# Moving the block boundary and the general-pass branch into the middle of the experts of a two-block transformer kernel

## What is computed

```python
h = _rms_norm(x, norm_mix[i])
z = h @ w_in[i]                      # q, k, v, conv inputs cu, cg, gates ga, gb
...
merged = jax.nn.sigmoid(ga) * y_a + jax.nn.sigmoid(gb) * y_b
x = x + merged @ w_out[i]
h2 = _rms_norm(x, norm_ffn[i])
x = x + _hier_moe(h2, ...)           # 32 experts, width 512, two of one group per token
g_ple = jax.nn.sigmoid(_rms_norm(x, norm_ple[i]) @ w_ple_gate[i])
x = x + g_ple * (p[i] @ w_ple_proj[i])
```

## Time and profile before

| | us |
|---|---|
| median of 3 runs | 2069.28 |
| lowest, highest | 2068.17, 2074.96 |
| profiled execution, its own time | 2068.92 |
| its span in the profile | 2066.8 |

### The profile page before, as it was taken

The page is one execution under the profiler, slowest core; times in us unless marked ns, Lnnn a source line. Parts: engine busy times, 40 slices in busy tenths (PEclk is TensorE's granted clock), DMA queues, the critical chain, the costliest instruction groups (busy, mean ns, idle before and its releaser), DMA issues. The chain is left out here.

```text
span 2066.8 us, 21051 instructions
## 1 busy us (share of the span) xinstructions
PE 1727.0 (84%) x9170; PEld 1120.7 (54%) x9170; DVE 545.8 (26%) x1109; ACT 335.2 (16%) x695; POOL 0.2 (0%) x4
## 2 busy tenths in 40 slices
PE   7999967666665899998666576679999999999999
PEld 6788522212221787883222122147888877888744
DVE  3853200000000376431000000025566333210000
ACT  2231200000000222310000000012152244210000
POOL 0000000000000000000000000000000000000000
PEclk9999987888888999999888878889999999999999
DMA  8436699999999634359999999981433333333441
GB/s 341 163 133 248 279 427 428 427 429 426 429 427 428 256 131 155 134 233 408 427 428 426 428 428 428 428 344 70 157 132 137 125 109 95 122 142 143 163 162 62
DMA packets 40175, 560.97 MB, mean 271 GB/s; under 512 B 4464, under 2 KB 4464, under 8 KB 5744
## 3 DMA queue, kind: packets, MB, share of 16 engines
q1 hardware_dynamic: 40080, 559.57, 66.7%
HBM read 558.50 MB, written 1.05 MB: 271 GB/s over the span
## 5 line engine op out<-in xcount | busy, mean ns | idle before, releaser
L1182 PE MATMUL ps<-ring,hB 128*32 128x512 f32 x1344 | 196.0, 712 | 119.7 <-DMA ring<-in_stream 119.7
L1574 PE MATMUL ps<-hA,ring 128*128 128x256 f32 (+1 forms) x1312 | 289.2, 382 | 0.6 <-DVE b_sc L2202 0.6
L1574 PEld LDWEIGHTS ps<-hA,ring 128*128 128x128 f32 (+1 forms) x1312 | 246.4, 188 | 42.2 <-issue 4.6
L563 PE MATMUL ps<-hA,ring 128*128 128x256 f32 x1152 | 253.0, 380 | 0.0
L563 PEld LDWEIGHTS ps<-hA,ring 128*128 128x128 f32 x1152 | 217.7, 190 | 32.7 <-issue 3.7
L1182 PEld LDWEIGHTS ps<-ring,hB 128*32 128x32 f32 x1344 | 41.7, 121 | 271.3 <-DMA ring<-in_stream 135.8
L1182 PE MATMUL ps<-l_extra,hB 128*32 128x512 f32 x704 | 117.5, 802 | 82.5 <-DMA l_extra<-in_stream 82.5
L1193 PE MATMUL ps<-ring,l_work 128*32 128x512 f32 x704 | 106.0, 736 | 55.7 <-DMA ring<-in_stream 47.2
L1274 DVE TENSOR_TENSOR l_work<-ps,l_work 128x512 f32<-128x512 f32 x16 | 11.1, 692 | 436.5 <-ACT l_work L1248 436.5
L1182 PEld LDWEIGHTS ps<-l_extra,hB 128*32 128x32 f32 x704 | 23.0, 128 | 163.5 <-DMA l_extra<-in_stream 93.4
L1836 PE MATMUL ps<-ring 128*128 128x512 f32 x256 | 110.0, 592 | 0.0
(11 more groups left out here) (317 smaller groups left out, 1696.3 us busy)
## 6 DMA issues: line engine op xcount, KB each, us to landing
ring<-in_stream SPq DMA_DIRECT2D x189, 2048.0 KB, 37.6
l_extra<-in_stream SPq DMA_DIRECT2D x64, 2048.0 KB, 40.8
ring<-in_stream SPq DMA_DIRECT2D x6, 1792.0 KB, 16.6
ring<-in_stream SPq DMA_DIRECT2D x4, 1344.0 KB, 7.9
ring<-in_stream SPq DMA_DIRECT2D x2, 1764.0 KB, 9.0
ring<-in_stream SPq DMA_DIRECT2D x2, 1024.0 KB, 29.8
b_bias<-in_bias SPq DMA_DIRECT2D x1, 2048.0 KB, 12.9
xT<-in_xT SPq DMA_DIRECT2D x1, 1024.0 KB, 4.8
```

What stands on the lines that cost most here:

```text
L563: mm = self.nc.tensor.matmul(out[:, m * T:(m + 1) * T], w[:, k, c * P:(c + 1) * P], src[:, k, :], start=(k == 0), stop=(k == kc - 1))
L1182: mm = nc.tensor.matmul(out[js, :], x_slots[q % 2][:, c, js], w[:, 0, j * D + n0:j * D + n0 + FF], start=(c == 0), stop=(c == DC - 1))
L1574: mm = nc.tensor.matmul(out[0:width, m * T:(m + 1) * T], w[:, k, (c0 + m) * width:(c0 + m + 1) * width], src[:, k, :], start=(k == 0), sto ...
```

## The change

The order of the program becomes: block 0 with the front of layer 0 and its quads 0 to 3; clear, load and branch; block 1 with the quads 4 to 7 and the PLE stage of layer 0, the front of layer 1 and its quads 0 to 3; clear, load and branch; block 2 with the rest of layer 1 and its PLE stage; clear; the second block of the model. There are as many boundaries as before. In detail:

- `SPLIT` is 4. `moe_tensor`, `moe_scalar` and `moe_vector` take a range of quads and a running number `n` for the semaphore counts within a block. At a boundary SP has issued the first eight slabs of the next quad and no more, since the two slots behind them serve `over_block` as scratch.
- The PLE slab stands in the stream ahead of the last four down slabs, and takes part in the cycle of the slots. The four banks of the projection are filled around and between the last down slabs, where the banks of gate and up are free.
- In the tail, VectorE adds the parts of the last `combine` and scales by the gain in turns; the first gate bank stands ahead of the mean square.
- A tenth slot, `late`, is made of scratch that is idle while the experts run: `hA` and the front's `raw` and `sig` share its memory. SP fills it for the first time once the four `htok` banks are filled.
- To make room, `work` shrinks from 5632 to 4096 columns: one buffer for the gathered tokens in place of two, silu and hidden values in one tile, slot results in `hB`. In the second block `kn` and `vn` use `late`, and 384 columns of parameters are loaded with the late ones. `over_block` uses one weight tile for gate, up and down in turn.

```diff
+LATE = RING + EXTRA
+CYCLE = LATE + 1
+SPLIT = QUADS // 2
+MOE_SLABS = QUADS * QUAD_SLABS
...
-        cycle = cycle[:3] + [RING + 1, cycle[3], RING + 2, RING] + cycle[4:]
+        cycle = cycle[:3] + [RING + 1, cycle[3], RING + 2, RING] + cycle[4:] + [LATE]
...
-        for m in range(QUADS * QUAD_SLABS):
-            s.add((l, "moe"), [cycle[m % len(cycle)]], P, 1, SLAB)
+        for m in range(MOE_SLABS):
+            if m == MOE_SLABS - FC:
+                s.add((l, "ple"), [cycle[m % CYCLE]], P, PLE // P, D, m0 + MOE_SLABS)
+            s.add((l, "moe"), [cycle[(m + (m >= MOE_SLABS - FC)) % CYCLE]], P, 1, SLAB, m0 + m)
...
     def ple_tensor(self, pe, claim, layer):
-        first = self.store.slabs.first
-        self.project(pe, claim, first[layer, "ple"], "ple", 0, self.pT)
+        first, store = self.store.slabs.first, self.store
+        i = first[layer, "ple_gate"]
+        w = store.wait(pe, i)
+        self.fill_bank(pe, claim, "ple_gate", 0, w, 0, self.hA, DC, self.scaled["ple"])
         self.mean_square(pe, claim, "ple")
-        for n in range(2):
-            self.project(pe, claim, first[layer, "ple_gate"] + n, "ple_gate", 2 * n, self.hA, self.scaled["ple"] if n == 0 else None)
+        self.fill_bank(pe, claim, "ple_gate", 1, w, 1, self.hA, DC)
+        store.free(i, self.filled["ple_gate"], 2)
+        self.project(pe, claim, i + 1, "ple_gate", 2, self.hA)
...
     def ple_vector(self, dve, step, layer, then_norm):
         vec = self.nc.vector
-        self.scale_by_gain(layer, "ple", range(DC))
+        added = 4 * (QUADS - SPLIT - 1)
+        for b in range(5):
+            if b < 4:
+                self.add_part(dve, added + b)
+            if b:
+                dve.wait_ge(self.part_added, added + b)
+                self.scale_by_gain(layer, "ple", range(2 * b - 2, 2 * b))
...
+            if q == QUADS - 1:
+                i = store.slabs.first[layer, "ple"]
+                w = store.wait(pe, i)
+                self.fill_bank(pe, claim, "ple", 0, w, 0, self.pT, PLE // P)
+            pe.wait_ge(self.hidT_ready, n + 1)
...
             for f in range(FC):
-                down(q, f)
-        combine(QUADS - 1)
+                down(q, n, f)
+                if q == QUADS - 1 and f < FC - 1:
+                    if f == 1:
+                        pe.wait_ge(self.put_copied, n + 1)
+                    self.fill_bank(pe, claim, "ple", f + 1, w, f + 1, self.pT, PLE // P)
+                    if f == FC - 2:
+                        store.free(i, self.filled["ple"], 4)
+        combine(n)
...
+                if tail:
                     inputs.wait_p(pe, layer - 1)
+                    self.moe_tensor(pe, layer - 1, SPLIT, QUADS, 0, claim)
                     self.ple_tensor(pe, claim, layer - 1)
...
+                if head:
+                    self.front_tensor(pe, claim, layer)
+                    self.moe_tensor(pe, layer, 0, SPLIT, n0)
...
+                    store.guard[next(i for i in range(m0, len(slabs.slot)) if slabs.slot[i] == LATE)] = (self.filled["htok"], 4)
+                    half = slabs.expert(layer, SPLIT * QUAD_SLABS)
+                    store.issue(sp, min(slabs.until(half - 1), half + CYCLE - 2))
```

More of the change, by code:

```diff
@@ L213, in __init__, with add @@
     def __init__(self):
-        self.slot, self.before, self.nth, self.shape, self.name = [], [], [], [], []
-        self.last = {s: None for s in range(RING + EXTRA)}
-        self.count = {s: 0 for s in range(RING + EXTRA)}
+        self.slot, self.before, self.nth, self.shape, self.at = [], [], [], [], []
+        self.last = {s: None for s in range(CYCLE)}
+        self.count = {s: 0 for s in range(CYCLE)}
         self.first = {}
-    def add(self, name, slots, rows, chunks, cols):
+    def add(self, name, slots, rows, chunks, cols, at=None):
         s = min(slots, key=lambda k: -1 if self.last[k] is None else self.last[k])
@@ L228, in add, with expert @@
         self.shape.append((rows, chunks, cols))
-        self.name.append(name)
+        self.at.append(i if at is None else at)
+    def expert(self, layer, m):
+        return self.first[layer, "moe"] + m + (m >= MOE_SLABS - FC)
     def until(self, consumed):
@@ L370, in __init__ @@
         self.extra = None
-        self.landed = [ctx.enter_context(nc.semaphore(f"landed{i}")) for i in range(RING + EXTRA)]
-        self.freed = []
+        self.late = late
+        self.guard = {}
+        self.landed = [ctx.enter_context(nc.semaphore(f"landed{i}")) for i in range(CYCLE)]
+        self.freed = {}
         self.issued = 0
@@ L391, in issue @@
                 sp.wait_ge(*self.freed[before])
-            sp.dma_start(self.slot(s)[0:rows, 0:chunks * cols], self.stream[i, 0:rows, 0:chunks * cols]).then_inc(self.landed[s], 16)
+            if i in self.guard:
+                sp.wait_ge(*self.guard[i])
+            sp.dma_start(self.slot(s)[0:rows, 0:chunks * cols], self.stream[self.slabs.at[i], 0:rows, 0:chunks * cols]).then_inc(self.landed[s], 16)
             self.issued += 1
@@ L652, in ple_vector @@
                 self.sum_bank(dve, step, "mix", b)
[L654 to L672, removed]
-                store.issue(sp, store.slabs.until(store.slabs.first["u_rnn"] - 1))
-        self.store.next_block()
     def front_tensor(self, pe, claim, layer):
@@ new lines, in gathered @@
+            act.wait_ge(self.put_filled, n + 1)
+            if n >= 2:
+                act.wait_ge(self.part_filled, 4 * (n - 1))
+            nc.scalar.copy(self.put[n % 2], ps[4][:, 0:T]).then_inc(self.put_copied, 1)
+        gathered(n0)
+        for q in range(q0, q1):
+            n = n0 + q - q0
+            act.wait_ge(self.slab_used, n * QUAD_SLABS + DC)
+            nc.scalar.activation(self.hid_slots, ps[0][:], ACT.Silu).then_inc(self.gu_silu, 1)
+            if q < q1 - 1:
+                gathered(n + 1)
+            act.wait_ge(self.turned_hid, n + 1)
@@ L1283, in layer_block, with block @@
+        if q1 < QUADS:
+            for b in range(4):
+                self.add_part(dve, 4 * n + b)
+    def block(self, layer, inputs):
+        store, slabs = self.store, self.store.slabs
+        head, tail = layer < DEPTH, layer > 0
+        n0 = QUADS - SPLIT if tail else 0
         with self.nc.Block(no_gpsimd_drain=True) as block:
@@ L1332, in over_block @@
         nc, store, ps = self.nc, self.store, self.ps
-        filled, emptied, hT = self.filled, self.emptied, self.hA
+        filled, emptied = self.filled, self.emptied
         m0 = store.slabs.first[layer, "moe"]
-        slabs = store.stream[m0:m0 + QUADS * QUAD_SLABS].rearrange("(q j) p n -> q j p n", j=QUAD_SLABS)
+        slabs = store.stream[m0:m0 + MOE_SLABS].rearrange("(q j) p n -> q j p n", j=QUAD_SLABS)
         ident = self.const[:, C_ID:C_ID + P]
-        def weights(j):
-            c = FC if j == 2 else DC
-            return store.extra[:, j].rearrange("p (c n) -> p c n", c=c)
+        half = store.slabs.expert(layer, SPLIT * QUAD_SLABS)
+        spare, own = (store.slot(store.slabs.slot[half + CYCLE - 1 - n]) for n in range(2))
+        hT = own[:, 0:DC * T].rearrange("p (c n) -> p c n", c=DC)
+        yacc = own[:, DC * T:].rearrange("p (t n) -> p t n", t=TT)
+        gate_w = spare.rearrange("p (c n) -> p c n", c=DC)
+        down_w = spare.rearrange("p (c n) -> p c n", c=FC)
         with nc.Block(no_gpsimd_drain=True) as block:
```

348 lines of the change are left out of this document (172 added, 176 removed).

## The result

The changed kernel takes 2037.32 us (median of 4 runs, 2033.01 to 2037.79) against 2069.24 for the kernel before (4 runs): a ratio of 0.9836, interval 0.9813 to 0.9858, or 32 us less. The forecast was 2031.6. The profiled execution took 2037.55 with a span of 2035.8 us, 31.0 less than before.

The account below looks back on a forecast made before the run. The weight stream bound the experts (864 us at 427 GB/s), TensorE the other long stretches. Gains 32.8 + 9.8 − 4.9 = 37.7 us off the profiled 2068.92 gave 2031.2, as a median 2031.6 us; range 2025 to 2047.

Parts of the forecast that it names:

- Part 1: Behind each layer's last slab: boundary and projection leave the tail, 50.6 to 34.2 us; gain 16.4 a layer, 32.8 us.
- Part 2: Before each layer's stream binds: a tenth slab moves while DMA stands idle; gain 2 × 4.9 = 9.8 us.
- Part 3: End of the expert stream: PLE slab ahead of the last four slabs costs 2 × 2.45 = 4.9 us.
- Part 4: In the expert stream: boundary behind the fourth quad, projection banks and fewer buffers are hidden, cost 0.
- my 13.2: Boundary behind the fourth quad: combine 4.9 plus a restart of 8.25 us, against 36.0 us of issued slabs.
- A: Rival, projection banks between last down slabs: slow clock delays the last slab, +19.6 over two layers, 2051 us; chance 0.13.
- B: Rival, tail: the 8.25 us gap belongs to the embedding code's start and stays, 2048 us; chance 0.07.
- C: Rival, stream start: the tenth slot brings nothing, some other slot or the guard is late, 2041 us; chance 0.05.
- D: Rival, boundary in mid-stream: SP held too long starves the DMA queue, 2088 us; chance 0.04 with milder forms.
- The rule on clock oscillation: Interleaved last down slabs: a loop that works briefly, then waits for DMA, falls back to slow clock; speaks for rival A.

Follow-up runs that it names:

- late guard: Changed kernel with the tenth slot's first load held until the first expert slab has been used: 2043.68 us, ratio 0.9874.
- the one profile without the branch: Changed kernel with load, branch and general pass left out: 2033.49 us, ratio 0.9817.
- one slab of cover: Changed kernel with SP allowed only one slab beyond the fourth quad ahead of the boundary in place of eight: 2055.02 us, ratio 0.9925.
- before without branch: Kernel before with load of the largest count, branch and general pass left out, barrier and clear kept: 2060.1 us, ratio 0.9955.
- a shift of 0.87 us: Changed kernel with one more pair of matmuls in the second block's first mean square: 2034.1 us, ratio 0.9821.
- four slabs of cover: Changed kernel with SP allowed four slabs ahead of the boundary in place of eight: 2034.5 us, ratio 0.9831.

## Why the prediction was right, and where it was off

- **Part 1, the tail.** Forecast 16.4 us a layer, measured 17.2 and 17.3. Gap, cold clock behind it and projection went as priced; VectorE's weave is what I had a little too dear: its last scaling ended at 670.18, +7.0 after the last slab, not +7.8. (The terms as written add up to +34.0, not +34.2.) The run with the projection moved back shows its share (6.9 a layer), that without the branch the boundary's (8.3 and 8.4, the 6.5 of load and branch among them).
- **Part 2, the tenth slot.** 4.9 us a layer, measured 5.1 and 4.8 with the late guard. SP issued the slab at 220.66; its transfer was not over by 228 but landed at 229.35, which cost nothing, as the stream starts again only at 232.
- **Part 3, the slab ahead.** 2.45 us a layer, measured 2.2 and 2.4.
- **Part 4, what is hidden.** SP's restart, which no row had shown, is 7.4 us after the last down slab in layer 0 and 9.1 in layer 1, inside my 13.2. The boundary itself cost nothing, and neither did the projection banks. The experts still took 0.9 and 1.3 us more than forecast, by a slab that is late near each layer's end; in the one profile without the branch this is gone, and its cause is open.
- **Rivals.** A: in layer 1 the first bank ran at the lower clock (3.58 us at 1326.27), the next three at the full clock, and the last slab was waited for. The down slabs between the banks took 1.92 us in both layers, the full clock's time, and only in the second profile of this kernel one took 2.94. B: the gap left the tail with the boundary. C: the late guard gives the 10.0 us back. D: its milder form shown with one slab of cover, absent with four or eight.
- **The step that failed** is the one that took the second block as it was. "In the second block 384 columns of parameters come later … 0, bound half a us" is right for these edits, but I took the kernel before's 647.6 us as that block's price, when it is the better of two: 647.4 to 648.6 where the clock stays, 650.4 to 653.3 where it falls. The profiled span, 2035.8, is 6.7 us over the forecast's 2029.1, and 5.1 of these are that (between forecast and median it is 5.7 in all); the range held it. Layer 1's front lost 1.1 us more, with the clock at 0.70 in 905 to 913, and of the 2.2 us that the experts took too long the tails made up 1.7. The rule on clock oscillation that I cited from the page TensorE: Matmul & The Clock Gate of the Trainium skill speaks of waits for DMA; here the clock fell with TensorE fully busy, which is not that case.

Whether the clock falls isn't decided by the edits of this change (before without branch falls, the late guard doesn't) nor by the length of the narrow stretch alone. With a shift of 0.87 us the profiled run kept it; but each kernel but one has a single profile, and the times of one kernel fall on both sides (2031.7 and 2037 to 2039 with four slabs of cover), so how often a kernel keeps it isn't known. What it is timed against stays open.

No version here beats the changed kernel beyond doubt. One pair of idle matmuls gave 2034.1, but by the place of the clock's fall, which any other edit may move again.

## What to carry to other kernels

A boundary with a load and a branch did not cost all engines the same: here TensorE stood idle for 8.25 us and VectorE for 2.0. Put it where another resource binds, and count the cover in transfers already issued: here four slabs (some 17 us) hid an SP absence of 7.8 us, one did not. Where the stream bound from some moment on, a transfer more ahead of that moment was worth its full length (4.9 us, measured 5.1 and 4.8), and one moved ahead of the last cost its full length (2.45 us, measured 2.2 and 2.4). And before a stretch's time is carried over unchanged, look whether TensorE's granted clock in it is a stable 1.00 or a near thing: it can move a kernel by 5 us with no instruction changed.

## What was not expected of the hardware

The granted clock fell to 0.50 in the midst of a stretch in which TensorE was busy 6.0 of 6.0 us, under narrow matmuls, in 9 of 14 profiles. It stayed in the profile with 0.87 us of added work ahead of it. With the same load and branch, TensorE's gap at a boundary was 2.7 us in some profiles and 6.7 to 8.9 in others. And with load and branch in mid-stream one of the last slabs of each layer was late by 0.6 to 1.5 us, in a stream at 427 GB/s and some 200 us behind the boundary; in the one profile without them none was.
